# Later loads in the first modulation, its scale and shift on ScalarE, and the spatial weights turned after the feature group

## The chip, the core and the metric

The kernel runs on one core of a Trainium2 chip. The metric is the device time of one execution in microseconds. An execution is one launch of one program, so everything below happens inside one timeline that the hardware profiler can record.

## What is computed

Two blocks run one after the other on a token matrix x of 512 tokens by 2048 features. Only the head of the first block matters here:

```python
cond = jax.nn.silu(c)
mod = cond @ w_ada[l] + b_ada[l]
shift, scale, gate = jnp.split(mod, 3, axis=-1)
h = rms_norm(x, norm_g[l]) * (1.0 + scale[:, None, :]) + shift[:, None, :]
z = h @ w_in[l]
u_a, v_a, g_a, q_b, k_b, v_b, g_b, f_b = jnp.split(z, pts, axis=-1)
y_a = chunked_spatial_gating(gelu(u_a), gelu(v_a), ln_v_g[l], ln_v_b[l], w_s[l], b_s[l]) * silu(g_a)
y_b = forgetting_attention(q_b, k_b, v_b, f_b, b_f[l]) * silu(g_b)
```

`chunked_spatial_gating` multiplies the normalised v_a by the lower triangle of `w_s` (8 heads of 128 by 128). All of this is float32.

## The kernel before

The program is written by hand for each engine. Engines meet at named semaphores, so the order of the code is the order on each engine. SyncE (SP in the profile) issues most loads, in order, into one DMA queue. GpSimd (POOL) issues the weights of the value features v_a. ScalarE (ACT) issues twelve small loads of vectors, the row loads, at the very start.

**Start.** x comes in by tokens. TensorE (PE) turns it by 128 by 128 transposes, ScalarE copies the result into `Y`, squares it, and TensorE sums the squares with a matrix of ones (`norm_squares`). VectorE (DVE) makes the variance from that, ScalarE takes Ln and Exp of it (`norm`), which gives the inverse deviation of every token (semaphore `deviation`).

**Four slabs.** Scale and shift of 2048 features are made in four slabs of 512. For one slab VectorE accumulates 16 blocks of `w_ada` of 512 KB, each times one element of silu(c) (`accumulate`, semaphore `acc_step`). The blocks pass through a ring of six slots in the `arena` (`start_in_0` to `start_in_5`). TensorE sums over the partitions (`reduce_slab`). VectorE turns that into columns (`slab_columns`). Then four tiles of x, already times the inverse deviation (`slab_normed`), get scale and shift (`slab_modulated`, semaphore `modulated`). TensorE multiplies each such tile by the value weights as soon as it is there (`value_product`), 32 float32 products for a slab, while VectorE accumulates the next slab. ScalarE rounds the tiles to `op_hi`, VectorE subtracts to get `op_lo` (`slab_low`): the later products run in three passes over these halves.

**Behind the slabs.** VectorE accumulates one more part of the modulation out of the same ring, 16 steps (`part_tile`), from 8 blocks of 512 KB. ScalarE rounds the first four weight tiles of the group f (a product 112 columns wide that holds the forget logits), and behind that applies Gelu to the value features, which empties the PSUM banks that f writes into. Then TensorE runs the group f, then q (two groups of 512 columns), k, v and the rest.

SyncE's queue around this place holds, in order: the last two `part_tile` blocks, `b_f`, a store of 4096 KB of x (`x_spill`), the bias `b_s`, and the weight blocks of f.

Constants come in one table `const` of 128 by 1408 floats. Its first 256 columns are the identity and the ones; the others, the triangles among them, are used later. `w_s`, its eight transposes and its mask (`tri_le`) stand inside slab 0, and so do the level masks (`masks`).

Of the kernel before, what the change touches and what calls it, by code (L numbers as in the profile page):

```python
# [5 lines left out]
P = 128  # L6
# [179 lines left out]
N_CONST = 7 * P + S  # L186

TMP = 0
AT_X_TOK, AT_START, AT_WS_RAW = 0, 8192, 16384
AT_RSTD_X, AT_PARK = 6144, 6656  # L190
START_RING, SLABS, SLAB = 6, 4, 4
AT_VA, AT_K, AT_V, AT_WST, AT_BS, AT_F, AT_FQ = 2048, 6144, 10240, 14336, 15360, 16384, 16896
# [15 lines left out]
class Build:  # L208
# [56 lines left out]
    def sem(self, name):  # L265
        if name not in self.sems:
            self.sems[name] = self.nc.alloc_semaphore(name)
        return self.sems[name]
# [21 lines left out]
def slab_input(B, slab):  # L290

    return B.at(TMP if slab % 2 else AT_VA, SLAB, S)
# [26 lines left out]
def sync_program(B, sp):  # L319
    A, sem, at = B.A, B.sem, B.at  # L320


    sp.dma_start(B.const[:, :], A["const"]).then_inc(sem("const_in"), 16)


    sp.dma_start(at(AT_X_TOK, NT, D), A["x"][0].rearrange("(n p) d -> p n d", p=P)).then_inc(sem("x_in"), 16)
# [3 lines left out]
    for n in range(SLABS * KT):  # L330
        slab, kt = divmod(n, KT)
        if n >= START_RING:

            sp.wait_ge(sem("acc_step"), n - START_RING + 1)
        sp.dma_start(ring[:, n % START_RING, :, :], w_ada[:, kt, 0:2, slab * GC:(slab + 1) * GC])\
            .then_inc(B.start_in[n % START_RING], 16)
        if n == 3:
            sp.dma_start(at(AT_WS_RAW, HEADS_A, P), A["w_s"][0].rearrange("h t s -> t h s")).then_inc(sem("ws_in"), 16)

            sp.dma_start(B.a_raw[:, :, :, :].rearrange("p a b c -> p (a b c)")[:, 0:len(LEVELS) * P],  # L340
                         A["masks"]).then_inc(sem("masks_in"), 16)
    w_part = A["w_ada"][0].rearrange("(k p) n -> p k n", p=P)
    c = GROUPS[FIRST["f"]]["part"] * GC
    for m in range(KT // 2):
        n = SLABS * KT + m
        if m < START_RING:

            sp.wait_ge(sem("acc_step"), n - START_RING + 1)
        else:

            sp.wait_ge(sem("part_tile"), 2 * (m - START_RING) + 2)
        sp.dma_start(ring[:, n % START_RING, :, :], w_part[:, 2 * m:2 * m + 2, c:c + GC])\
            .then_inc(B.start_in[n % START_RING], 16)
    sp.dma_start(B.bf[96:112, :], A["b_f"].rearrange("o h -> h o")).then_inc(sem("bf_in"), 16)

    sp.wait_ge(sem("x_turned"), KT)
# [240 lines left out]
def pool_program(B, pool):  # L597
    nc, sem, at = B.nc, B.sem, B.at

    pool.wait_ge(sem("acc_step"), 6)  # L600
    for b in range(4 * SLABS):
        g, kt = va_block(b)
        if b >= RAW:

            pool.wait_ge(sem("va_used"), b - RAW + 1)
        pool.dma_start(B.w_raw[:, b % RAW, :, :],
                       B.weight(GROUPS[g])[:, kt:kt + 2, GROUPS[g]["col"]:GROUPS[g]["col"] + GC])\
            .then_inc(B.va_in[b % RAW], 16)

    queries = at(AT_QST, 2, S)  # L610

    pool.wait_ge(sem("mixing"), HEADS_A)
    for h in range(HEADS_B):
        rows, others = (slice(DH_B * (x % 2), DH_B * (x % 2 + 1)) for x in (h, h + 1))
        if h < 2:
            nc.gpsimd.memset(queries[others, h, :], 0.0)
        if h >= 2:

            pool.wait_ge(sem("scores"), 4 * (h - 1) + 1)
        nc.gpsimd.tensor_copy(queries[rows, h % 2, :], B.Y[rows, 8 + h // 2, :])  # L620
        nc.gpsimd.drain().then_inc(sem("queries_in"), 1)

    n = FIRST["wo1"]

    pool.wait_ge(B.bank_free[n % 2], n // 2 + 1)
    nc.gpsimd.memset(at(AT_WGC, 1, 2048)[0:33, 0, :], 0.0)
    nc.gpsimd.drain()
    nc.gpsimd.memset(B.arena[32:33, AT_RC:AT_RC + SC], 1.0)
    nc.gpsimd.drain()
    nc.gpsimd.memset(B.small[0:1, 95:96], 0.0).then_inc(sem("gates_cleared"), 1)  # L630

    pool.wait_ge(sem("states_out"), 1)
    nc.gpsimd.memset(at(AT_WG, 1, 512)[0:33, 0, :], 0.0)
    nc.gpsimd.drain()
    nc.gpsimd.memset(B.arena[32:33, AT_RT:AT_RT + S], 1.0)
    nc.gpsimd.drain()
    nc.gpsimd.memset(B.small[0:1, 95:96], 0.0).then_inc(sem("gates_cleared"), 1)
# [36 lines left out]
def scalar_program(B, act):  # L674
# [273 lines left out]
    for slab in range(SLABS):  # L948
        for t in range(SLAB):
            k = SLAB * slab + t  # L950
            act.wait_ge(sem("modulated"), k + 1)
            Act(B.op_hi[:, k, :], slab_input(B, slab)[:, t, :], ACT.Copy).then_inc(sem("op_high"), 1)
    for c in range(4):
        high_tile(c, GROUPS[FIRST["f"]]["width"])

# [327 lines left out]
def tensor_program(B, pe):  # L1283
# [262 lines left out]
    for t in range(KT):  # L1546
# [2 lines left out]
        for j in range(NT):  # L1549
            last = turn(ps[:, 1 + t % 4, j * P:(j + 1) * P], x_tok[:, j, t * P:(t + 1) * P])  # L1550
        last.then_inc(sem("turned"), 1)
    pe.wait_ge(sem("ws_in"), 16)
    for h in range(HEADS_A):
        last = turn(ps[:, 5 + h // 4, h % 4 * P:(h % 4 + 1) * P], at(AT_WS_RAW, HEADS_A, P)[:, h, :])
    last.then_inc(sem("ws_turned"), 1)
    norm_squares()

    def reduce_slab(slab):
# [15 lines left out]
                  B.w_raw[:, b % RAW, k, :], start=t % SLAB == 0 if own else t == 0,  # L1574
                  stop=t % SLAB == SLAB - 1 if own else t == KT - 1)

    pe.wait_ge(sem("ws_masked"), 1)
    reduce_slab(0)
    for slab in range(SLABS):

# [21 lines left out]

    F = FIRST
    group(F["f"])
    run(F["q"], 1)
    run(F["k"], 1)
    run(F["v"], 1)
    mixer_tensor(B, pe, reduce_parts)
# [237 lines left out]
def vector_program(B, dve):  # L1846
# [401 lines left out]
    def slab_columns(slab):  # L2248


        dve.wait_ge(sem("start_summed"), slab + 1)
        k = SLAB * slab
        bias = B.vec[:, VEC["b_ada"]:VEC["b_ada"] + 32].rearrange("p (v c) -> p v c", v=2)[:, :, k:k + SLAB]
        mod = B.mod[:, 0:32].rearrange("p (v c) -> p v c", v=2)[:, :, k:k + SLAB]
        V.tensor_tensor(mod, ps[:, 7, 0:2 * SLAB].rearrange("p (v c) -> p v c", v=2), bias, ALU.add)
        V.drain()
        V.scalar_tensor_tensor(out=B.mod[:, 16 + k:16 + k + SLAB], in0=B.mod[:, 16 + k:16 + k + SLAB], scalar=1.0,
                               in1=B.vec[:, VEC["norm_g"] + k:VEC["norm_g"] + k + SLAB], op0=ALU.add, op1=ALU.mult)
        V.drain()

    def slab_normed(slab):

# [3 lines left out]
        V.tensor_tensor(slab_input(B, slab), Y[:, SLAB * slab:SLAB * slab + SLAB, :],  # L2266
                        at(AT_RSTD_X, 1, S).to_broadcast([P, SLAB, S]), ALU.mult)
        V.drain()

    def slab_modulated(slab):  # L2270
        x = slab_input(B, slab)
        for t in range(SLAB):
            k = SLAB * slab + t
            V.tensor_scalar(x[:, t, :], x[:, t, :], B.mod[:, 16 + k:17 + k], B.mod[:, k:k + 1],  # L2274
                            ALU.mult, ALU.add).then_inc(sem("modulated"), 1)

    def slab_low(slab, t):
        k = SLAB * slab + t
# [16 lines left out]
    for n in range(SLABS * KT):  # L2295
        slab, kt = divmod(n, KT)
        accumulate(n)
        if slab == 0:
            if kt == 9:
                dve.wait_ge(sem("ws_turned"), 1)  # L2300
                V.tensor_tensor(at(AT_WST, HEADS_A, P), ps[:, 5:7, :].rearrange("p b (h t) -> p (b h) t", t=P),
                                B.tri_le.unsqueeze(1).to_broadcast([P, HEADS_A, P]), ALU.mult).then_inc(sem("ws_masked"), 1)
            if kt == 11:
                dve.wait_ge(sem("masks_in"), 16)
                V.tensor_copy(B.masks[:, :, :].rearrange("p l c -> p (l c)"),
                              B.a_raw[:, :, :, :].rearrange("p a b c -> p (a b c)")[:, 0:len(LEVELS) * P])\
                    .then_inc(sem("masks_made"), 1)
            if kt == 12:
                dve.wait_ge(sem("squares_summed"), 4)
                V.tensor_scalar(at(AT_RSTD_X, S), ps[:, 7, :], 1.0 / D, EPS, ALU.mult, ALU.add)\  # L2310
                    .then_inc(sem("variance"), 1)
            if kt == 14:
                dve.wait_ge(sem("deviation"), 1)
                slab_normed(0)
        else:
            if kt == 1:
                slab_columns(slab - 1)
                slab_modulated(slab - 1)
            if kt in (4, 5, 6, 7):
                slab_low(slab - 1, kt - 4)  # L2320
            if kt == 15:
                park(slab - 1)
                slab_normed(slab)
    slab_columns(SLABS - 1)
    slab_modulated(SLABS - 1)
    for t in range(SLAB):
        slab_low(SLABS - 1, t)

    for t in range(KT):
        part_tile(FIRST["f"], t)  # L2330
    park(SLABS - 1)

    def scaled(m):
# [11 lines left out]
    for n, g in enumerate(GROUPS):  # L2345
# [22 lines left out]
        if name == "f":  # L2368

            for k in range(FIRST["va"], FIRST["va"] + 2):  # L2370
                dve.wait_ge(B.bank_free[k % 2], k // 2 + 1)
            stats = B.small[:, 16:16 + 48].rearrange("p (a s) -> p a s", s=12)
            for b in range(NT):
                for h in range(2):
                    V.bn_stats(stats[:, b, 6 * h:6 * h + 6], va[:, b, h * GC:(h + 1) * GC])
            V.drain()
            for b in range(NT):
                V.bn_aggr(B.small[:, 64 + 2 * b:66 + 2 * b], stats[:, b, :])
            V.drain()
            mv = B.small[:, 64:72].rearrange("p (a b) -> p a b", b=2)  # L2380
            V.tensor_scalar(B.small[:, 0:4], mv[:, :, 1], EPS, None, ALU.add).then_inc(sem("value_variance"), 1)
        if name == "q" and i == 0:
            dve.wait_ge(sem("value_deviation"), 1)
            V.reciprocal(B.small[:, 4:8], B.small[:, 0:4])
# [431 lines left out]
```

## Time and profile before

| | us |
|---|---|
| median of 3 runs | 2897.32 |
| lowest and highest of them | 2896.2, 2901.43 |
| the profiled execution's own time | 2894.05 |
| span of its trace | 2892.3 |
| TensorE busy in the span | 2774.3 |
| VectorE busy | 1791.3 |
| ScalarE busy | 1047.8 |

The span runs from the first to the last instruction of the program in the trace; the time of the execution has a little around it. All later times are microseconds from the start of the span. In a row of the timeline the first number is the start, the second the duration of the row (it can hold several instructions, xN), and the brackets at the end say how long the engine was idle before it and what ended that. A `q` behind an engine's name means its sequencer, that is, the issue of a transfer.

### The profile page before, as it was taken

How to read it: one execution, taken by the hardware profiler on the slowest of the kernel's cores; microseconds unless marked ns; L12 is line 12 of the kernel's file. 1: busy time of each engine (PE TensorE's matmuls, PEld its weight loads, DVE VectorE, ACT ScalarE, POOL GpSimd, SP SyncE). 2: the span in 40 equal slices, each digit the busy share in tenths (PEclk: the TensorE clock that was granted, in tenths of full speed). 3: DMA queues.
4: the chain of work that ended last, by engine and by line, in shares of the span. 5: the costliest groups of instructions: out<-in, count | busy, mean ns of one | idle time of the engine just before them, and what ended most of it. 6: DMA issues, size and time to landing. Idle time of an engine off the chain costs nothing.

```text
span 2892.3 us, 35101 instructions
## 1 busy us (share of the span) xinstructions
PE 2774.3 (96%) x12345; PEld 2198.7 (76%) x12345; DVE 1791.3 (62%) x2747; ACT 1047.8 (36%) x1633; POOL 27.4 (1%) x44
## 2 busy tenths in 40 slices
PE   6999999999999989999999999999999899999996
PEld 3468887777788866788877778787788688888884
DVE  6856675555698757455564738483977776335454
ACT  3032222444332364422243534443422622234224
POOL 0000000000000000000000000000000000000000
PEclk9999999999999999999999999999999999999998
DMA  9966552222466647466522322235566365333341
GB/s 344 356 211 216 190 190 90 79 75 73 145 205 201 221 139 255 142 212 194 193 69 88 95 79 87 73 94 179 192 228 218 108 212 189 95 99 99 124 124 58
DMA packets 240189, 451.25 MB, mean 156 GB/s; under 512 B 23848, under 2 KB 45818, under 8 KB 235436
## 3 DMA queue, kind: packets, MB, share of 16 engines
q1 hardware_dynamic: 237236, 440.80, 46.4%
q0 software_dynamic: 2304, 8.39, 0.8%
q8 instruction: 86, 1.41, 0.2%
q14 instruction: 59, 0.48, 0.1%
q10 hardware_dynamic: 504, 0.17, 0.0%
HBM read 422.01 MB, written 27.30 MB: 155 GB/s over the span
## 4 chain that ended last, share of the span: by engine, by line
PE 74%; issue 13%; DVE 5%; ACT 2%; DVEq 2%; DMA 1%; ACTq 1%; SPq 1%; POOLq 0%; POOL 0%
PE ps L1345 18%; PE ps L1348 18%; PE ps L1351 18%; PE ps L1573 3%; PE ps L1801 2%; PE ps L1358 1%; PE ps L1364 1%; PE ps L1361 1%; PE ps L1718 1%; PE ps L1709 1%; PE ps L1832 1%; PE ps L1835 1%; PE ps L1315 1%; PE ps L1320 1%; PE ps L1317 1%
## 5 line engine op out<-in xcount | busy, mean ns | idle before, releaser
L1345 PE MATMUL ps<-op_hi,w_hi 128*128 128x512 f32 (+2 forms) x2800 | 782.8, 399 | 21.2 <-ACT op_hi L926 8.2
L1858 DVE TENSOR_TENSOR w_lo<-w_raw,w_hi 128x512 fp32r<-128x512 f32 (+2 forms) x672 | 440.6, 661 | 555.0 <-ACT w_hi L688 307.5
L1351 PE MATMUL ps<-op_hi,w_lo 128*128 128x512 f32 (+2 forms) x2800 | 756.3, 390 | 4.4 <-DVE w_lo L1858 4.4
L1348 PE MATMUL ps<-op_lo,w_hi 128*128 128x512 f32 (+2 forms) x2800 | 759.5, 391 | 0.0
L1345 PEld LDWEIGHTS ps<-op_hi,w_hi 128*128 128x128 f32 (+1 forms) x2800 | 519.7, 190 | 138.2 <-issue 23.2
L1351 PEld LDWEIGHTS ps<-op_hi,w_lo 128*128 128x128 f32 (+1 forms) x2800 | 527.8, 189 | 116.2 <-DVE w_lo L1858 5.6
L1348 PEld LDWEIGHTS ps<-op_lo,w_hi 128*128 128x128 f32 (+1 forms) x2800 | 529.8, 189 | 112.7 <-issue 0.3
L688 ACT ACTIVATE w_hi<-w_raw 128x512 fp32r<-128x512 f32 (+2 forms) x416 | 242.8, 592 | 607.2 <-PE ps L1351 446.9
L713 ACT ACTIVATE w_hi<-w_raw 128x512 fp32r<-128x512 f32 x288 | 181.8, 632 | 580.9 <-PE ps L1351 451.4
L1881 DVE SCALAR_TENSOR_TENSOR acc<-a_raw,vec,acc 128x512 f32<-128x512 f32 x525 | 381.5, 745 | 15.3 <-DMA a_raw<-in_w_ada 12.3
L2586 DVE TENSOR_TENSOR w_lo<-w_raw,w_hi 128x512 fp32r<-128x512 f32 x128 | 83.5, 686 | 63.8 <-ACT w_hi L1208 58.4
L1358 PE MATMUL ps<-w_hi,op_hi 128*128 128x512 f32 x384 | 111.6, 399 | 4.2 <-ACT w_hi L688 4.2
L1573 PE MATMUL ps<-w_raw,arena 128*128 128x512 f32 x256 | 112.4, 600 | 1.1 <-DVE arena L2274 1.1
L1364 PE MATMUL ps<-w_lo,op_hi 128*128 128x512 f32 x384 | 109.2, 393 | 2.7 <-DVE w_lo L1858 2.6
L1361 PE MATMUL ps<-w_hi,op_lo 128*128 128x512 f32 x384 | 108.6, 391 | 0.0
L1573 PEld LDWEIGHTS ps<-w_raw,arena 128*128 128x128 f32 x256 | 49.0, 193 | 61.4 <-issue 59.4
L2510 DVE TENSOR_TENSOR w_lo<-w_raw,w_hi 128x512 fp32r<-128x512 f32 x64 | 44.3, 692 | 76.1 <-ACT w_hi L1116 76.1
L1244 ACT ACTIVATE arena<-arena 128x2048 f32<-128x2048 f32 x28 | 53.6, 1915 | 101.5 <-DVE arena L2639 101.5
L1358 PEld LDWEIGHTS ps<-w_hi,op_hi 128*128 128x128 f32 x384 | 71.5, 189 | 23.1 <-ACT w_hi L688 5.5
L1208 ACT ACTIVATE w_hi<-w_raw 128x512 fp32r<-128x512 f32 x128 | 75.3, 621 | 36.1 <-PE ps L1351 36.1
L1364 PEld LDWEIGHTS ps<-w_lo,op_hi 128*128 128x128 f32 x384 | 71.8, 188 | 20.3 <-DVE w_lo L1858 5.4
L1361 PEld LDWEIGHTS ps<-w_hi,op_lo 128*128 128x128 f32 x384 | 72.4, 189 | 15.6
(279 smaller groups left out, 2413.8 us busy)
## 6 DMA issues: line engine op xcount, KB each, us to landing
a_raw<-in_w_ada SPq DMA_DIRECT2D x216, 512.0 KB, 4.0
w_raw<-in_w_in_e SPq DMA_DIRECT2D x160, 512.0 KB, 4.7
w_raw<-in_w_in SPq DMA_DIRECT2D x96, 512.0 KB, 4.8
arena<-in_w_ada SPq DMA_DIRECT2D x72, 512.0 KB, 6.9
w_raw<-in_w_in_o SPq DMA_DIRECT2D x64, 512.0 KB, 4.3
w_raw<-in_w_out SPq DMA_DIRECT2D x32, 512.0 KB, 4.9
w_raw<-in_w_out_e SPq DMA_DIRECT2D x32, 512.0 KB, 5.0
w_raw<-in_w_out_o SPq DMA_DIRECT2D x32, 512.0 KB, 3.8
```

Of the source, the lines that this page charges most:

```text
L688: Act(B.w_hi[:, c % RING, 0:width], B.w_raw[:, raw, c % 2, 0:width], ACT.Copy).then_inc(sem("hi_done"), 1)
L713: Act(B.w_hi[:, t % RING, 0:width], B.w_raw[:, raw, t % 2, 0:width], ACT.Copy).then_inc(sem("hi_done"), 1)
L1345: mm(ps[0:m, bank + j, 0:tok], hi[:, cols], B.op_hi[:, k, 0:tok], start=first, stop=False)
L1348: mm(ps[0:m, bank + j, 0:tok], hi[:, j * P:j * P + m], B.op_lo[:, k, 0:tok], start=False, stop=False)
L1351: last = mm(ps[0:m, bank + j, 0:tok], lo[:, j * P:j * P + m], B.op_hi[:, k, 0:tok], start=False, stop=last_t)
L1358: mm(ps[:, bank + j, :], B.op_hi[:, k, rows], hi, start=first, stop=False)
L1361: mm(ps[:, bank + j, :], B.op_lo[:, k, j * P:j * P + P], hi, start=False, stop=False)
L1364: last = mm(ps[:, bank + j, :], B.op_hi[:, k, j * P:j * P + P], lo, start=False, stop=last_t)
L1573: return mm(ps[:, 4 * g + j, :], slab_input(B, slab)[:, t % SLAB, j * P:(j + 1) * P], B.w_raw[:, b % RAW, k, :], start=t % SLAB == 0 if ow ...
L1858: V.tensor_tensor(B.w_lo[:, c % RING, 0:width], B.w_raw[:, c // 2 % RAW, c % 2, 0:width], B.w_hi[:, c % RING, 0:width].bitcast(f32), ALU.s ...
L1881: last = V.scalar_tensor_tensor(out=sums, in0=x, scalar=col, in1=sums, op0=ALU.mult, op1=ALU.add)
L2586: V.tensor_tensor(B.w_lo[:, c % RING, :], B.w_raw[:, c // 2 % RAW, c % 2, :], B.w_hi[:, c % RING, :].bitcast(mybir.dt.float32), ALU.subtract)\
```

## The change

Four things are changed. (1) Of `const` only the first 256 columns come first; `masks`, the rest of `const` and `w_s` are issued behind the eight `part_tile` blocks, and `w_s` waits on SyncE for the tenth `part_tile`, since it now lies in a slot of the ring. (2) GpSimd issues the third and fourth value weight block of the first slab only after eleven accumulations. (3) Scale and shift of the slab tiles go from VectorE to ScalarE, in the same instruction stream as the rounding. (4) The transposes of `w_s` stand between f and q on TensorE, its mask on VectorE behind the statistics of the value features, and the copy of the level masks behind the `part_tile` steps.

```diff
@@ sync_program
-    sp.dma_start(B.const[:, :], A["const"]).then_inc(sem("const_in"), 16)
+    sp.dma_start(B.const[:, 0:2 * P], A["const"][:, 0:2 * P]).then_inc(sem("const_in"), 16)
...
-        if n == 3:
-            sp.dma_start(at(AT_WS_RAW, HEADS_A, P), A["w_s"][0].rearrange("h t s -> t h s")).then_inc(sem("ws_in"), 16)
-
-            sp.dma_start(B.a_raw[:, :, :, :].rearrange("p a b c -> p (a b c)")[:, 0:len(LEVELS) * P],
-                         A["masks"]).then_inc(sem("masks_in"), 16)
...
+    sp.dma_start(B.a_raw[:, :, :, :].rearrange("p a b c -> p (a b c)")[:, 0:len(LEVELS) * P],
+                 A["masks"]).then_inc(sem("masks_in"), 16)
+    sp.dma_start(B.const[:, 2 * P:], A["const"][:, 2 * P:]).then_inc(sem("const_rest_in"), 16)
+
+    sp.wait_ge(sem("part_tile"), 10)
+    sp.dma_start(at(AT_WS_RAW, HEADS_A, P), A["w_s"][0].rearrange("h t s -> t h s")).then_inc(sem("ws_in"), 16)
     sp.dma_start(B.bf[96:112, :], A["b_f"].rearrange("o h -> h o")).then_inc(sem("bf_in"), 16)
@@ pool_program
+        if b == 2:
+            pool.wait_ge(sem("acc_step"), 11)
@@ scalar_program
             k = SLAB * slab + t
-            act.wait_ge(sem("modulated"), k + 1)
-            Act(B.op_hi[:, k, :], slab_input(B, slab)[:, t, :], ACT.Copy).then_inc(sem("op_high"), 1)
+            x = slab_input(B, slab)[:, t, :]
+            if t == 0:
+                act.wait_ge(sem("slab_ready"), slab + 1)
+            Act(x, x, ACT.Identity, scale=B.mod[:, 16 + k:17 + k], bias=B.mod[:, k:k + 1]).then_inc(sem("modulated"), 1)
+            nc.scalar.drain()
+            Act(B.op_hi[:, k, :], x, ACT.Copy).then_inc(sem("op_high"), 1)
@@ tensor_program
-    pe.wait_ge(sem("ws_in"), 16)
-    for h in range(HEADS_A):
-        last = turn(ps[:, 5 + h // 4, h % 4 * P:(h % 4 + 1) * P], at(AT_WS_RAW, HEADS_A, P)[:, h, :])
-    last.then_inc(sem("ws_turned"), 1)
...
-    run(F["q"], 1)
+
+    pe.wait_ge(sem("const_rest_in"), 16)
+    pe.wait_ge(sem("ws_in"), 16)
+    for h in range(HEADS_A):
+        last = turn(ps[:, 1 + h // 4, h % 4 * P:(h % 4 + 1) * P], at(AT_WS_RAW, HEADS_A, P)[:, h, :])
+    last.then_inc(sem("ws_turned"), 1)
+    group(F["q"])
+    pe.wait_ge(sem("ws_masked"), 1)
+    group(F["q"] + 1)
@@ vector_program
-            if kt == 9:
-                dve.wait_ge(sem("ws_turned"), 1)
-                V.tensor_tensor(at(AT_WST, HEADS_A, P), ps[:, 5:7, :].rearrange("p b (h t) -> p (b h) t", t=P),
-                                B.tri_le.unsqueeze(1).to_broadcast([P, HEADS_A, P]), ALU.mult).then_inc(sem("ws_masked"), 1)
...
             if kt == 1:
                 slab_columns(slab - 1)
-                slab_modulated(slab - 1)
...
+            dve.wait_ge(sem("const_rest_in"), 16)
+            dve.wait_ge(sem("ws_turned"), 1)
+            V.tensor_tensor(at(AT_WST, HEADS_A, P), ps[:, 1:3, :].rearrange("p b (h t) -> p (b h) t", t=P),
+                            B.tri_le.unsqueeze(1).to_broadcast([P, HEADS_A, P]), ALU.mult).then_inc(sem("ws_masked"), 1)
```

On SyncE, this is what is issued from the `part_tile` blocks of the ring on, before the change; the brackets hold the semaphores that an issue waits for.

```order
L352 DMA arena<-in_w_ada 128x2x512 [waits part_tile] x2
L354 DMA bf<-in_b_f 16x1
L357 DMA x_spill<-Y 128x8192 [waits x_turned]
L534 DMA arena<-in_b_s 128x1024 [waits acc_step]
L377 DMA w_raw<-in_w_in 128x2x112 [waits va_used] x4
```

And this is the same place after the change.

```order
L347 DMA arena<-in_w_ada 128x2x512 [waits part_tile] x2
L349 DMA a_raw<-in_masks 128x896
L351 DMA const<-in_const 128x1152
L354 DMA arena<-in_w_s 128x8x128 [waits part_tile]
L355 DMA bf<-in_b_f 16x1
L358 DMA x_spill<-Y 128x8192 [waits x_turned]
L535 DMA arena<-in_b_s 128x1024 [waits acc_step]
L378 DMA w_raw<-in_w_in 128x2x112 [waits va_used] x4
```

Three loads have moved in ahead of the store `x_spill` and of the weights of f, and one of the three holds a wait of its own, behind which all the others stand.

On ScalarE, this is the handling of a slab's tiles and what follows the last one, before the change.

```order
L952 ACTIVATE op_hi<-arena 128x512 [waits modulated] x16
L688 ACTIVATE w_hi<-w_raw 128x112 [waits weights_in_0]
...
L688 ACTIVATE w_hi<-w_raw 128x112 [waits weights_in_1]
...
L972 ACT_TABLE_LOAD
L972 ACTIVATE arena<-ps 128x4x512 [waits va_used]
```

After the change one slab reads like this on ScalarE (three more slabs follow, then the same rows for w_hi and the Gelu).

```order
L957 ACTIVATE arena<-arena,mod 128x512 [waits slab_ready]
L959 ACTIVATE op_hi<-arena 128x512
L957 ACTIVATE arena<-arena,mod 128x512
L959 ACTIVATE op_hi<-arena 128x512
L957 ACTIVATE arena<-arena,mod 128x512
L959 ACTIVATE op_hi<-arena 128x512
L957 ACTIVATE arena<-arena,mod 128x512
L959 ACTIVATE op_hi<-arena 128x512
```

Sixteen instructions have come over to ScalarE, each followed by a drain and the rounding of the same tile; the Gelu still stands behind the first weight tiles of f.

## Rows read from the trace of the kernel before

**Rows 1.** The page: busy time of each engine and its share.

```profile
PE 2774.3 (96%) x12345; PEld 2198.7 (76%) x12345; DVE 1791.3 (62%) x2747; ACT 1047.8 (36%) x1633; POOL 27.4 (1%) x44
```

**Rows 2.** The timeline from the start to the first value product.

```profile
6.54 5.28 SPq L338 DMA_DIRECT2D arena<-in_w_s  x1
...
16.18 0.81 PE L1289 MATMUL ps<-const,Y 128*128 128x128 f32 x3 [16.18 <-DMA Y<-in_pool_scale]
...
16.79 10.19 PE L1289 MATMUL ps<-const,arena 128*128 128x128 f32 x72
...
29.12 14.00 PE L1440 MATMUL ps<-arena,const 128*128 128x512 f32 x32 [2.14 <-ACT arena L809]
...
33.67 1.22 DVE L2301 TENSOR_TENSOR arena<-ps,const 128x1024 f32<-128x1024 f32 x1
...
43.16 0.69 DVE L2310 TENSOR_SCALAR arena<-ps 128x512 f32<-128x512 f32 x1
...
44.59 2.67 DVE L2245 SCALAR_TENSOR_TENSOR acc<-arena,vec,acc 128x1024 f32<-128x1024 f32 x2 [0.73 <-DMA arena<-in_w_ada]
45.86 0.63 ACT L816 ACTIVATE arena<-arena 128x512 f32<-128x512 f32 x1
47.18 2.28 DVE L2266 TENSOR_TENSOR arena<-Y,arena 128x2048 f32<-128x2048 f32 x1
...
50.99 3.54 PE L1302 MATMUL ps<-const,acc 128*128 128x1 f32 x16 [7.87 <-DVE acc L2245]
...
55.66 4.80 PE L1573 MATMUL ps<-w_raw,arena 128*128 128x512 f32 x7 [1.13 <-DVE arena L2274]
```

**Rows 3.** Busy time by stretch: engines, granted clock, DMA share, GB/s.

```profile
20.00:40.00 20.00, 17.86 (x84) 11.64 (x84) 14.52 (x12) 15.71 (x20) 3.01 (x4) 1.00 1.06 379
...
55.66:82.19 26.53, 26.52 (x59) 11.78 (x60) 23.52 (x23) 2.18 (x4) 2.17 (x3) 0.94 0.89 315
```

**Rows 4.** The second slab in the timeline; the groups of 0 to 250 us.

```profile
83.89 27.71 PE L1573 MATMUL ps<-w_raw,arena 128*128 128x512 f32 x64
...
L2274 DVE TENSOR_SCALAR arena<-arena,mod 128x512 f32<-128x512 f32 x16 | 7.7, 542 | 0.3
```

**Rows 5.** The timeline of ScalarE and TensorE at a later modulation.

```profile
2272.76 0.81 ACT L924 ACTIVATE arena<-Y,mod 128x512 f32<-128x512 f32 x1 [2.38 <-DVEq L2136]
...
2274.27 0.81 ACT L924 ACTIVATE arena<-Y,mod 128x512 f32<-128x512 f32 x1
...
2274.42 2.04 PE L1345 MATMUL ps<-op_hi,w_hi 128*128 128x512 f32 x4 [8.19 <-ACT op_hi L926]
2276.26 1.63 PE L1348 MATMUL ps<-op_lo,w_hi 128*128 128x512 f32 x4
```

**Rows 6.** The timeline from the last slab to group f, one DMA issue among it.

```profile
144.89 2.49 DVE L1995 TENSOR_TENSOR op_lo<-arena,op_hi 128x512 fp32r<-128x512 f32 x4
...
147.90 12.72 DVE L1881 SCALAR_TENSOR_TENSOR acc<-arena,vec,acc 128x512 f32<-128x512 f32 x15
...
151.31 0.42 SPq L357 DMA_DIRECT2D x_spill<-Y  x1
...
w_raw<-in_w_in SPq DMA_DIRECT2D x1, 112.0 KB, 15.7
...
167.92 0.85 ACT L688 ACTIVATE w_hi<-w_raw 128x112 fp32r<-128x112 f32 x4 [22.09 <-DMA w_raw<-in_w_in]
...
170.09 1.88 ACT L972 ACTIVATE arena<-ps 128x2048 f32<-128x2048 f32 x1
...
172.12 0.79 PE L1345 MATMUL ps<-op_hi,w_hi 128*112 128x512 f32 x1
```

**Rows 7.** The timeline of TensorE and VectorE in the first group of q.

```profile
185.32 1.15 PE L1345 MATMUL ps<-op_hi,w_hi 128*128 128x512 f32 x4 [1.63 <-issue]
...
196.95 0.69 DVE L1858 TENSOR_TENSOR w_lo<-w_raw,w_hi 128x512 fp32r<-128x512 f32 x1
...
198.10 1.07 PE L1351 MATMUL ps<-op_hi,w_lo 128*128 128x512 f32 x4
```

More of the change, by code:

```diff
@@ L188 @@
 TMP = 0
-AT_X_TOK, AT_START, AT_WS_RAW = 0, 8192, 16384
+AT_X_TOK, AT_START, AT_WS_RAW = 0, 8192, 10240
 AT_RSTD_X, AT_PARK = 6144, 6656
@@ L1575, in value_product @@
                   stop=t % SLAB == SLAB - 1 if own else t == KT - 1)
-    pe.wait_ge(sem("ws_masked"), 1)
     reduce_slab(0)
@@ L2258, in slab_columns @@
                                in1=B.vec[:, VEC["norm_g"] + k:VEC["norm_g"] + k + SLAB], op0=ALU.add, op1=ALU.mult)
-        V.drain()
+        V.drain().then_inc(sem("slab_ready"), 1)
     def slab_normed(slab):
@@ L2268, in slab_normed @@
         V.drain()
[L2270 to L2275, printed above, removed]
     def slab_low(slab, t):
@@ L2298, in vector_program @@
         if slab == 0:
-            if kt == 9:
-                dve.wait_ge(sem("ws_turned"), 1)
-                V.tensor_tensor(at(AT_WST, HEADS_A, P), ps[:, 5:7, :].rearrange("p b (h t) -> p (b h) t", t=P),
-                                B.tri_le.unsqueeze(1).to_broadcast([P, HEADS_A, P]), ALU.mult).then_inc(sem("ws_masked"), 1)
[L2303 to L2307, printed above, removed]
             if kt == 12:
@@ L2324, in vector_program @@
     slab_columns(SLABS - 1)
-    slab_modulated(SLABS - 1)
     for t in range(SLAB):
@@ L2330, in vector_program @@
         part_tile(FIRST["f"], t)
+    dve.wait_ge(sem("masks_in"), 16)
+    V.tensor_copy(B.masks[:, :, :].rearrange("p l c -> p (l c)"),
+                  B.a_raw[:, :, :, :].rearrange("p a b c -> p (a b c)")[:, 0:len(LEVELS) * P])\
+        .then_inc(sem("masks_made"), 1)
     park(SLABS - 1)
```

## The prediction, made before the changed kernel was run

> **What bounds the kernel now.** I read the page first, to see whose time counts. TensorE is busy for 96% of the span [rows 1], so a change at the head can only move the end if it moves TensorE's work or opens a gap in it. The timeline of the head then shows where TensorE waits. It waits for the row loads until 16.18. It transposes x with no idle time ahead, so x had landed. From 29.12 it sums the squares for 14.00 us, and from 43.12 it idles 7.87 us until the last accumulation of slab 0 is done [rows 2]. Its first value product starts at 55.66 [rows 2]. From there on it does not stop: a slab takes 27.71 us of products with nothing between [rows 4], until the group f at 172.12 [rows 6].
>
> Two places therefore decide: the start of the products (55.66), and the start of f, which needs two things at once, the end of the products and the Gelu (170.09 plus 1.88 is 171.97). The Gelu stands on ScalarE behind four weight tiles of f, and ScalarE waited 22.09 us for those weights [rows 6]. Both conditions are met in the same microsecond before the change. So f has no slack on either side: products that end sooner bring nothing unless the weights of f come sooner, and later weights cost in full.
>
> **The start of the products.** `const` shrinks from 1408 to 256 columns of floats: 128 x 1152 x 4 bytes, 0.59 MB, no longer travel ahead of x. At 379 GB/s [rows 3] that is 1.5 us. The rest that leaves the head (`masks`, `w_s`) was queued behind x and the first four blocks and does not touch x.
>
> The chain from x to the variance is serial: transposes, copies, squares, sums (14.00), variance at 43.16, and Exp until 46.49 (45.86 plus 0.63). All of it shifts by 1.5, so Exp would end at 44.99. VectorE's own side: from the variance (43.16) to `slab_normed` (47.18) it spent 4.02 us, of which 0.73 waited for a block [rows 2]. With blocks that land sooner this is 3.3, so from 41.66 it is ready at about 45.0. Both give 45.1 in place of 47.18, a gain of 2.1. The mask of `w_s` (1.22 us at 33.67 [rows 2]) and the copy of the masks leave VectorE in a stretch where it would wait for the sums of squares anyway. They gain nothing, and the same holds for the eight transposes of `w_s`: the squares on ScalarE end after them. Were the sums of squares not in the way, the accumulations alone could be done some 10 us sooner; they are in the way.
>
> GpSimd's new wait holds two blocks of value weights back until the eleventh accumulation. The eleventh is due near 34 us (from about 18, at 2.67/2 each [rows 2], with a little for the first two blocks of weights beside them), and the two are needed 14 us (half of 27.71) into the first slab, near 68. I cost it at nothing; the 34 us between are the cover.
>
> A point of doubt is whether the row loads move too, since TensorE waited for them, not for x. They are twelve small loads, and they were still under way while 4 MB of x passed. I take it that they are slow because they share the engines with x, so that they end sooner when x does. If they stay at 16.18, nothing ahead of Exp moves, and the gain is only VectorE's wait: 47.18 less 46.49, 0.7. The Trainium skill, DMA: Bandwidth & Descriptors, section "Issuing engines are not separate DMA queues", says that loads from all issuing engines run on the same 16 DMA engines and interleave. By that rule the row loads move with x, and the sum stays as I have it.
>
> **Scale and shift on ScalarE.** VectorE took 542 ns for a tile [rows 4]. The same form on ScalarE, Identity with a scale and a bias from the modulation table, takes 0.81 us, and with the drain and the rounding a tile comes every 1.51 us (2272.76 to 2274.27) [rows 5]. TensorE waits for the first tile of slab 0, so this costs 0.27 there: the first product starts at 55.66 - 2.1 + 0.27 = 53.8. In the later slabs TensorE still has three products of the old slab (six records of 27.71/64 = 0.43, 2.6 us) while the columns are made, so 0.27 is mostly hidden; I take 0.1 for each of three. A tile every 1.51 us is enough, since TensorE works 3.5 us on one (8 records). So the products end 1.5 us sooner than before (2.1 - 0.27 - 0.3). The Trainium skill, ScalarE: Activation LUTs, section "Rules for kernel authors", says that add and mul belong on VectorE and not on ScalarE. By that rule the move costs and brings nothing; the rows make it 0.27 at the start and the next item behind the last slab.
>
> VectorE is freed of 4 x 0.54 us a slab, but it is not the bound in the slabs: TensorE is. After the last slab it is worse off. `slab_low` ended at 147.38 (144.89 plus 2.49) [rows 6]. Now its fourth tile waits for ScalarE. The columns are ready at about 143.0, since the old modulated tiles began there (144.89 less 3 x 0.54, rounded down for the overlap). The fourth rounding ends 3 x 1.51 + 0.81 + 0.07 + 0.63 = 6.0 us later, at 149.1, and 0.7 of subtraction follows: 149.8. So `part_tile` starts 2.4 us later relative to the products.
>
> **The queue ahead of f.** This is the large term. Before, SyncE issued `x_spill` at 151.31, and the weights of f came 16.6 us later, at 167.92, behind 4 MB of `x_spill` and 0.5 MB of `b_s` in the same queue [rows 6]. Now SyncE waits for ten `part_tile` steps first. The fifteen steps after the first took 12.72 us from 147.90, 0.85 each, so the tenth ended at 147.90 + 9 x 0.85 = 155.5; with the 2.4 us it is 157.9. Then `w_s`, `b_f` and `x_spill` are issued, each at about 0.45: `x_spill` at 158.8, which is 7.5 us later. `masks` and the rest of `const` (1.05 MB, 2.8 us at 379 GB/s) go into the queue near 153 and are through by then. What stands ahead of f's weights is then one block of 0.5 MB (`w_s` in place of the last block of `w_ada`), `x_spill` and `b_s`, the same bytes as before. So f's weights come 16.6 us after `x_spill` again: 7.5 us later relative to the products. The lower end is 5, if the store runs faster with the queue to itself. The upper end comes from `w_s`: its issue took 5.28 us at the head [rows 2], where the queue was full; if that were the issue's own cost, 7.5 would be 12.
>
> Rounding, table load and Gelu follow unchanged, so f starts at 172.12 + 7.5 - 1.5 = 178.1. TensorE has meanwhile idled some 7 to 8 us. After a gap of 8.19 us at 2274.42 the first four products took 2.04 us and the next four 1.63 [rows 5], against 1.07 in the steady run [rows 7]: 1.5 us lost to the lower clock. In slab 0 the granted clock was 0.94 over 26.53 us [rows 3], 12% of it at half speed, 1.6 lost. I add 1.5, with 0 to 1.6 as ends for its size.
>
> **Between f and q.** TensorE idled 1.63 us before q at 185.32 [rows 7], waiting for weights that are issued at f's pace, so this gap moves along. Eight transposes (10.19/72 = 0.14 each, 1.1 us [rows 2]) fit into it; `w_s` landed long before. Without that cover they would cost 1.1. The mask, 1.22 us, now precedes the low tile that VectorE starts at 196.95 and ends at 197.64. TensorE needs it at 198.10 [rows 7]: slack 0.46, so 0.76 is lost. The copy of the masks lies in a stretch in which VectorE has nothing to do.
>
> **The sum**, against the profiled execution's 2894.05: -1.5 (products sooner) + 7.5 (f's weights) + 1.5 (clock) + 0.8 (mask) = +8.3, which gives 2902.4. The median of the runs is 2897.32, 3.3 above the profiled one, so I predict 2905.6.
>
> **Rivals.**
> (a) The store absorbs most of it. If the 4 MB drain sooner and the clock stays up, the terms are -2 + 5 + 0 + 0.5 = +3.5: 2901. For it: the queue is emptier when the store is issued. Against: the same bytes took 16.6 us.
> (b) The weights of f do not gate, and only the head counts: -1.5 + 0.8 = -0.7, 2896.6. Against it stands ScalarE's wait of 22.09 us that ended on just these weights.
> (c) Faster. The sums of squares do not hold the first slab, and the accumulations set the start, 10 us sooner, and VectorE's lead pulls `part_tile` along: -10 - 1.5 + 7.5 - 2 = -6, 2891. It decides when the variance is ready before 35 us; 14.00 us of products after 27 speak against it.
> (d) The issue of `w_s` costs 5 us by itself: +13, 2910.
> (e) The row loads stay at 16.18: the gain at the start shrinks by 1.4 and the sum becomes +9.7, 2907.
>
> **Chances.** The forecast 0.47, (e) 0.13, (d) 0.09, (a) 0.18, (b) 0.09, (c) 0.04. A measurement tells 0.2%, 5.8 us, from no change. Slower by more than that: the forecast, (d) and (e), less a little for the forecast's lower edge: 0.66. Within: (a), (b) and that edge, 0.29. Faster: 0.05. The range from 2898 to 2912 leaves out (b) and (c) and the far end of (d).
>
> **What the profile would show.** First value product near 53.8, with its modulated tile from ScalarE at 0.81 us each. No new wait in slabs 1 to 3. `x_spill` issued near 157.3 (158.8 less 1.5). A gap on TensorE of 7 to 8 us before f, ended by the Gelu, with the clock at its lower level behind it. A short wait of TensorE for a low tile in the first q group. I am wrong if f starts before 174, or if f's weights come clearly less than 16.6 us after `x_spill` is issued.

## The result and the profile after

The changed kernel took 2908.68 us (median of 6 runs, 2905.67 to 2909.66), the kernel before 2898.16 (6 runs, 2896.04 to 2903.93): a ratio of 1.0027, 95% interval 1.0017 to 1.0037. It is slower by 7.8 us by the ratio (0.0027 x 2898) and by 10.5 by the medians; forecast were 2905.6 and 8.3. The profiled execution after took 2905.67 at a span of 2903.9, against 2894.05 at 2892.3.

The first two groups are the page after, busy time of each engine, and the timeline of TensorE and ScalarE from the start to the first value product.

```profile
PE 2781.0 (96%) x12345; PEld 2199.8 (76%) x12345; DVE 1784.4 (61%) x2731; ACT 1060.9 (37%) x1649; POOL 27.4 (1%) x44
```

```profile
15.29 0.81 PE L1296 MATMUL ps<-const,Y 128*128 128x128 f32 x3 [15.29 <-DMA Y<-in_pool_scale]
...
27.84 14.00 PE L1447 MATMUL ps<-arena,const 128*128 128x512 f32 x32 [3.09 <-ACT arena L812]
...
49.01 3.58 PE L1309 MATMUL ps<-const,acc 128*128 128x1 f32 x16 [7.17 <-DVE acc L2255]
53.10 0.81 ACT L957 ACTIVATE arena<-arena,mod 128x512 f32<-128x512 f32 x1 [7.89 <-DVEq L2269]
53.97 28.22 PE L1576 MATMUL ps<-w_raw,arena 128*128 128x512 f32 x58 [1.38 <-ACT arena L957]
```

The row loads ended 0.89 sooner than in [rows 2], the sums of squares began 1.28 sooner, and the first value product stands at 53.97 in place of 55.66: the head gave 1.7. It was soon lost. Busy time by stretch, after (in a row: the stretch and its length; busy us and instructions of PE, PEld, DVE, ACT and POOL; granted clock; DMA share; GB/s):

```profile
46.00:60.00 14.00, 9.61 (x23) 6.01 (x24) 11.65 (x13) 5.45 (x8) 0.00 (x0) 0.52 0.78 251
53.97:82.03 28.06, 28.06 (x59) 12.25 (x60) 21.56 (x20) 4.64 (x7) 2.17 (x3) 0.89 0.94 325
```

The same stretch before:

```profile
46.00:60.00 14.00, 7.88 (x23) 5.51 (x24) 11.75 (x14) 2.69 (x5) 0.00 (x0) 0.63 0.82 287
```

The clock has two levels, full and half, so a granted clock of 0.52 over 14 us is 13.4 us at the lower one (2 x 0.48 x 14), and 0.63 is 10.4. The products start sooner and run slower, so the first slab, 26.53 us in [rows 3], takes 28.06, and the lead is down to 0.15. Nothing stalls in slabs 1 to 3; the last column sums begin at 140.55 (140.69 before).

This belongs to the one execution and not to the change. Four kernels below have the same code up to this place. All four read 0.63 in this stretch, as before; in three the last column sums begin at 138.66, 138.93 and 139.57, and only the fourth lost its lead too (140.83), in its sums of squares, which took 15.70 us in place of 14.00.

Now the part that decides. The timeline after, from the last slab to q, of TensorE, ScalarE, VectorE and the issues on SyncE:

```profile
140.55 1.84 PE L1309 MATMUL ps<-const,acc 128*128 128x1 f32 x16
142.91 0.81 ACT L957 ACTIVATE arena<-arena,mod 128x512 f32<-128x512 f32 x1 [22.45 <-DVEq L2269]
148.05 0.63 ACT L959 ACTIVATE op_hi<-arena 128x512 fp32r<-128x512 f32 x1
148.71 0.69 DVE L2005 TENSOR_TENSOR op_lo<-arena,op_hi 128x512 fp32r<-128x512 f32 x1 [0.72 <-ACT op_hi L959]
149.90 12.72 DVE L1891 SCALAR_TENSOR_TENSOR acc<-arena,vec,acc 128x512 f32<-128x512 f32 x15
152.81 0.46 SPq L349 DMA_DIRECT2D a_raw<-in_masks  x1
153.32 0.43 SPq L351 DMA_DIRECT2D const<-in_const  x1
157.52 0.38 SPq L354 DMA_DIRECT2D arena<-in_w_s  x1
158.69 0.42 SPq L358 DMA_DIRECT2D x_spill<-Y  x1
159.65 25.49 SPq L378 DMA_DIRECT2D w_raw<-in_w_in  x8
175.30 0.85 ACT L691 ACTIVATE w_hi<-w_raw 128x112 fp32r<-128x112 f32 x4 [26.63 <-DMA w_raw<-in_w_in]
177.47 1.88 ACT L979 ACTIVATE arena<-ps 128x2048 f32<-128x2048 f32 x1
179.40 0.77 PE L1352 MATMUL ps<-op_hi,w_hi 128*112 128x512 f32 x1 [6.86 <-ACT arena L979]
192.33 1.03 PE L1296 MATMUL ps<-const,arena 128*128 128x128 f32 x8
193.64 1.16 PE L1352 MATMUL ps<-op_hi,w_hi 128*128 128x512 f32 x4 [0.28 <-issue]
```

ScalarE's last rounding ends at 148.68 and `part_tile` starts at 149.90, 2.0 later than in [rows 6]. SyncE stands from 153.75 (the issue of `const`) to 157.52 for the tenth `part_tile`. `x_spill` goes out at 158.69 and f's weights reach ScalarE at 175.30, 16.6 us later, as before (151.31 to 167.92). TensorE idles 6.86 ahead of f, and q starts 8.32 later than in [rows 7]. The issues of the stretch 150 to 161, with the time from issue to landing:

```profile
x_spill<-Y SPq DMA_DIRECT2D x1, 4096.0 KB, 14.6
arena<-in_w_ada SPq DMA_DIRECT2D x2, 512.0 KB, 5.4
const<-in_const SPq DMA_DIRECT2D x1, 576.0 KB, 8.6
arena<-in_w_s SPq DMA_DIRECT2D x1, 512.0 KB, 6.0
...
a_raw<-in_masks SPq DMA_DIRECT2D x1, 448.0 KB, 7.7
w_raw<-in_w_in SPq DMA_DIRECT2D x1, 112.0 KB, 15.6
```

`masks` landed at 160.5 and the rest of `const` at 161.9, not ahead of the store but about 2 and 3 us behind its issue. Behind q the difference between the two traces wanders between 8.3 and 14.7 us, in both directions, at steps where the granted clock changes in the one and not in the other, and ends at 11.6.

In the tables below, "to f" and "to q" are the times from the start of the last column sums to the first product of f and of q; this takes the head, and what its clock did, out of the comparison. "Gap" is TensorE's idle time ahead of f. Each ratio is against the kernel before, measured beside the kernel in question. Before: 31.43 to f (172.12 - 140.69), 44.63 to q. After: 38.85 and 53.09, gap 6.86.

### The profile page after: what moved, and what is told of

Its sections match the earlier page's. It is cut to its first block, busy times and chain, and to the rows that moved or that the text cites. A ratio compares the mean times of both kernels' runs of the same rounds, so it can differ in the third digit from the quotient of the medians.

```text
span 2903.9 us, 35121 instructions
## 1 busy us (share of the span) xinstructions
PE 2781.0 (96%) x12345; PEld 2199.8 (76%) x12345; DVE 1784.4 (61%) x2731; ACT 1060.9 (37%) x1649; POOL 27.4 (1%) x44
## 4 chain that ended last, share of the span: by engine, by line
PE 85%; DVE 5%; ACT 3%; issue 2%; DMA 2%; ACTq 2%; DVEq 2%; SPq 0%
PE ps L1352 21%; PE ps L1355 20%; PE ps L1358 20%; PE ps L1576 3%; PE ps L1365 2%; PE ps L1371 2%; PE ps L1368 2%; PE ps L1811 2%; PE ps L1845 1%; PE ps L1842 1%; PE ps L1322 1%; PE ps L1327 1%; PE ps L1324 1%; PE ps L1728 1%; PE ps L1719 1%
## 5 line engine op out<-in xcount | busy, mean ns | idle before, releaser
L1891 DVE SCALAR_TENSOR_TENSOR acc<-a_raw,vec,acc 128x512 f32<-128x512 f32 x525 | 381.3, 745 | 17.9 <-DMA a_raw<-in_w_ada 15.3
```

The lines of the kernel that those rows point to most:

```text
L1891: last = V.scalar_tensor_tensor(out=sums, in0=x, scalar=col, in1=sums, op0=ALU.mult, op1=ALU.add)
```

## The experiments

Two causes could make f's weights late, and the expectations weigh them. One is the wait, the step of the prediction: SyncE stands for the tenth `part_tile` and all behind it stands too. The other is the bytes: `masks`, the rest of `const` and `w_s`, 1.5 MB, now travel between the last blocks and f's weights, and a store issued sooner would end no sooner. A third part is ScalarE's tiles, which start `part_tile` later.

**The wait behind the store** (changed kernel; `w_s` and its wait go behind `x_spill` and `b_s`).

```diff
-    sp.wait_ge(sem("part_tile"), 10)
-    sp.dma_start(at(AT_WS_RAW, HEADS_A, P), A["w_s"]...)
     ...  # b_f, x_spill, b_s
+    sp.wait_ge(sem("part_tile"), 10)
+    sp.dma_start(at(AT_WS_RAW, HEADS_A, P), A["w_s"]...)
```

> The changed kernel with w_s and its wait for the tenth part_tile moved behind x_spill and b_s in SyncE's order. Theory A (the wait on SyncE holds the store back, and f's weights with it): x_spill is issued right after the rest of const, near 154.7 instead of 158.7; masks, the rest of const and w_s (1.5 MB) are still ahead of f's weights, so these land near 173 instead of 175.3, f starts near 177, and the time falls by 1.5 to 3 us from 2908.7. Theory B (the bytes of the three loads in the queue are the whole cost, the wait is harmless): f's weights land at 175 as before and the time does not move.

Ratio 1.0029 (1.0019 to 1.0038): nothing gained. The issues of its stretch 145 to 165:

```profile
x_spill<-Y SPq DMA_DIRECT2D x1, 4096.0 KB, 17.8
...
w_raw<-in_w_in SPq DMA_DIRECT2D x1, 112.0 KB, 17.9
```

The store was issued at 154.54, 4.15 sooner, and took 17.8 us in place of 14.6, so it landed only 0.9 sooner (172.3 and 173.3). `w_s`, issued at 157.80 and now behind it, landed 17.9 us later, at 175.7, and f's weights right behind at 176.1. It was 39.42 to f. Without the wait the bytes hold f, and the wait as the one cause has fallen.

**The store early** (changed kernel; `x_spill` is issued ahead of the last two `part_tile` blocks, where SyncE would next wait for a slot of the ring).

```diff
+        if m == START_RING:
+            sp.wait_ge(sem("x_turned"), KT)
+            sp.dma_start(B.x_sp, B.Y[:, :, :]).then_inc(sem("spilled"), 16)
...
-    sp.wait_ge(sem("x_turned"), KT)
-    sp.dma_start(B.x_sp, B.Y[:, :, :]).then_inc(sem("spilled"), 16)
```

> The changed kernel with the 4 MB store x_spill issued before the seventh part_tile block, near 136, in place of behind w_s. Theory A (f's weights behind the store are the whole loss of about 8 us): f's weights land before 166, the idle time of TensorE before f goes to about 0, the clock stays at its full level there, and the time is 2898 to 2900, about that of the kernel before. Rival C (ScalarE's modulated tiles and the later mask cost several us by themselves): f starts on time but the time stays above 2903. Rival D (the store takes the DMA engines from the value weights of the last slab): a wait of TensorE for w_raw inside slab 3 of several us.

Ratio 1.0002 (0.9991 to 1.0013). Its timeline at the end of SyncE's program for the slabs:

```profile
150.92 0.47 SPq L352 DMA_DIRECT2D a_raw<-in_masks  x1
...
155.64 0.38 SPq L357 DMA_DIRECT2D arena<-in_w_s  x1
...
157.36 18.03 SPq L379 DMA_DIRECT2D w_raw<-in_w_in  x8
```

The wait and the 1.5 MB are still there, but 4 MB no longer stand behind them. f's first weights were issued at 157.36 and reached ScalarE at 162.69, well ahead of need. f started with no gap ahead of it, 32.37 to f: 6.5 of the 7.4 us are back, and the ratio is clear of that of the changed kernel. So nearly all the loss lies in when the store's bytes leave.

Of the 0.94 that is left, 0.70 is a new wait inside the last slab, the expectation's rival D in small. TensorE waited for a block of value weights, which GpSimd had issued at 134.95, 0.6 behind the store (134.34), and which took 15.7 us to land:

```profile
150.76 20.84 PE L1577 MATMUL ps<-w_raw,arena 128*128 128x512 f32 x48 [0.70 <-DMA w_raw<-in_w_in]
...
167.00 0.48 ACT L692 ACTIVATE w_hi<-w_raw 128x112 fp32r<-128x112 f32 x2 [3.82 <-DMA w_raw<-in_w_in]
```

The second row shows a condition of f that the prediction does not have: ScalarE needs four weight tiles of f ahead of the Gelu, and the third and fourth came only at 167.00. The next experiment shows why.

**The same on the kernel before**, a control: does an early store help by itself?

> The kernel before with the same early store and nothing else. By theory A f had no slack before but was not late either, so the time is that of before within 1 us (2897 to 2899): the products still end at 172. If it is several us faster, the store gated something in the kernel before as well; if slower, the store costs where it now stands, and e2 has to be read with that.

Ratio 1.0002 (0.9994 to 1.0011), 31.42 to f. It does not. The first two tiles came early, at 162.84, and the other two as before: 27.33 us behind the column sums (169.31 - 141.98), against 27.23 in the kernel before, where all four were taken at 167.92.

```profile
169.31 0.48 ACT L689 ACTIVATE w_hi<-w_raw 128x112 fp32r<-128x112 f32 x2 [5.99 <-DMA w_raw<-in_w_in]
```

Their load goes into a slot that the value products free. What SyncE waits for between 120 and 200 us says so, here in the kernel before:

```profile
SPq L377 <- PE ps L1573: 18.2, 2, 12.2
```

So with the store out of the way the products set f twice over: directly, and by this slot. The early store repairs what the change broke, and nothing else.

**Scale and shift back on VectorE** (changed kernel; `slab_modulated` returns to VectorE, which is not shown in the cut).

```diff
-            if t == 0:
-                act.wait_ge(sem("slab_ready"), slab + 1)
-            Act(x, x, ACT.Identity, scale=B.mod[:, 16 + k:17 + k], bias=B.mod[:, k:k + 1])...
-            nc.scalar.drain()
-            Act(B.op_hi[:, k, :], x, ACT.Copy).then_inc(sem("op_high"), 1)
+            act.wait_ge(sem("modulated"), k + 1)
+            Act(B.op_hi[:, k, :], slab_input(B, slab)[:, t, :], ACT.Copy).then_inc(sem("op_high"), 1)
```

> The changed kernel with scale and shift of the slab tiles back on VectorE. Theory A: the first product starts 0.2 us sooner, part_tile starts 1.9 us sooner behind the last slab, so x_spill and f's weights come 1.9 us sooner, and the time falls by about 2 us, to 2906 to 2907. Rival: if VectorE's relief in the slabs mattered, a wait of TensorE appears in slabs 1 to 3 and the time rises.

Ratio 1.0021 (1.0011 to 1.0031). 36.10 to f, 2.75 less than after. The store went out at 155.26, measured from the column sums 2.2 sooner than after (15.94 against 18.14). The tiles on ScalarE thus cost 2.75 of the 7.4 us, 2.2 of it in the place that the prediction named. This rests on the traces: the intervals of the two ratios (1.0021 and 1.0027) overlap. No new wait appeared in slabs 1 to 3, so VectorE's relief was worth nothing there.

**The loads ahead** (changed kernel; `masks` and the rest of `const` ahead of the last two blocks, the wait stays), and **both** (with the edit of the first experiment too).

```diff
+        if m == START_RING:
+            sp.dma_start(B.a_raw...[:, 0:len(LEVELS) * P], A["masks"]).then_inc(sem("masks_in"), 16)
+            sp.dma_start(B.const[:, 2 * P:], A["const"][:, 2 * P:]).then_inc(sem("const_rest_in"), 16)
...
-    sp.dma_start(B.a_raw...[:, 0:len(LEVELS) * P], A["masks"]).then_inc(sem("masks_in"), 16)
-    sp.dma_start(B.const[:, 2 * P:], A["const"][:, 2 * P:]).then_inc(sem("const_rest_in"), 16)
```

> The changed kernel with masks and the rest of const issued ahead of the seventh part_tile block, where the DMA engines were idle (145 to 150 us); w_s, its wait and x_spill stay. Measured from the last column sum (L1309, slab 3) to f's first product, which takes out what the clock did earlier: 31.4 us in the kernel before, 38.9 in the changed one. Theory B (the 1.5 MB more in the queue are the whole delay): 1.05 MB less at some 300 GB/s, f 3.5 us sooner, 35.4. Theory AB (the bytes and SyncE's wait each bind by themselves, so that removing one shows the other): x_spill is still issued near 158.7 and f's weights come 15 to 16.6 us later, 37.5 to 38.9.

> e5 and e1 together: masks and the rest of const ahead, the wait and w_s behind x_spill and b_s. Both theories leave only w_s (0.5 MB) and ScalarE's late tiles (part_tile 1.9 us later): f's weights 3.7 us sooner than in the changed kernel, 35.1 us from the last column sum to f, and a gap of TensorE of 3 to 4 us. If it stays near 38 to 39, neither the bytes nor the wait are the cause.

The loads ahead alone: 1.0024 (1.0015 to 1.0033), 37.18 to f. Both: 1.0011 (1.0002 to 1.0021), 35.59. In the first the store was issued at 156.95 behind the wait, 18.0 us behind the column sums as after (18.14), and took 13.3. So the wait removed alone gives nothing, the loads removed alone 1.7, both 3.3. Of these 3.3 us the bytes by themselves hold all, the wait by itself half: the expectation that each binds alone (37.5 to 38.9 to f) was nearly met.

**All three** (both, and scale and shift on VectorE).

> The changed kernel with the three repairs that leave the store where it is: masks and the rest of const ahead of the last blocks, w_s and its wait behind the store, scale and shift on VectorE. From the start of the last column sums to the first product of f it took 31.43 us before the change, 38.85 after it, 35.59 with the first two repairs, 36.10 with the third alone. If ScalarE's later tiles and the queue add up (they held up the store one behind the other), this is 35.6 less 2.75, near 32.8, where the 1.4 left is w_s ahead of f's weights, and the ratio is near 0.9995. If ScalarE's part was only the wait for the tenth step, which is gone from this place already, it stays near 35.6 and the ratio near 1.001.

Ratio 0.9999 (0.9990 to 1.0008), 33.43 to f: 5.4 of the 7.4 us are back, where 3.3 and 2.75 make 6.0, so the parts nearly add. The store now left when it did before, 10.63 us behind the column sums against 10.62, and took 14.7 us. Most of the 2.0 left is `w_s`, which now stands between `b_s` and f's weights: `b_s` landed at 166.0 (149.94 + 16.1) and `w_s` at 167.8 (153.67 + 14.1), 1.7 us apart.

**VectorE for the tiles, and the store early.**

> The changed kernel with the early store of e2 and scale and shift back on VectorE. f's weights are early in both, so ScalarE's later tiles cost only 0.24 us at the first product and nothing behind the last slab: 31.4 to 32.4 us from the last column sum to f as in e2, and the time of e2 within 1 us (2898). If it is 2 us or more faster than e2, the move to ScalarE costs in a place not seen.

> The fastest kernel again, on one chip with the one beside it: scale and shift on VectorE and the store ahead of the last blocks. If its first result was its time and not chance, ratio 0.9987 with 0.001 to either side, and 31.4 us from the last column sums to f.

2896.3 (2892.19 to 2899.03) against 2899.78, ratio 0.9987 (0.9978 to 0.9996), the fastest of all. The repeat gave 2895.88 and 0.9991 (0.9981 to 1.0001). It was 31.43 and 31.42 to f. This version keeps the head's gain and pays nothing for it; that it beats the kernel before by about 0.1% is likely, though the repeat's interval just reaches 1. Its expectation took 2 us or more over the early store alone as a sign that the tiles on ScalarE cost in a place not seen. The medians are 2.2 apart (2898.5 and 2896.3), but of different sets, and the intervals overlap, so the times do not decide it. The traces show 0.94 to f: TensorE's wait of 0.70 in the last slab is gone. The likely reason is the order of two issues: with the store early alone the store went out 0.6 us ahead of that block of value weights, which took 15.7 us; here it went out 1.1 and 1.7 us behind it (136.64 behind 135.53, and 137.10 behind 135.35), and the block took 8.4 and 7.6. The first products, in the repeat's timeline:

```profile
49.10 3.58 PE L1306 MATMUL ps<-const,acc 128*128 128x1 f32 x16 [7.18 <-DVE acc L2252]
53.80 2.93 PE L1573 MATMUL ps<-w_raw,arena 128*128 128x512 f32 x3 [1.13 <-DVE arena L2281]
```

**The same with seven more products behind the sums of squares**, to keep TensorE busy in its idle stretch; their result isn't used.

```diff
     norm_squares()
+    for _ in range(7):
+        mm(ps[:, 0, :], B.ones, at(AT_SQ, S), start=True, stop=True)
```

> e7 with seven more 128x512 products of the ones on TensorE behind the sums of squares (their result is overwritten): they fill 6 of the 7.2 idle us before the first column sum. If the lower clock there is what cost 3 to 5 us (column sum 3.57 for 1.84, slab 0 at 0.94 or less), the clock stays at its full level, the column sum takes 1.8 us, and slab 0 ends 3 to 4 us sooner: about 2895. If the clock is lowered all the same, no change against e7.

Ratio 0.9993 (0.9984 to 1.0002), the same as without them, so neither branch of the expectation came: the lower clock did not go away, and it was not unchanged. Its stretch was shorter:

```profile
49.00:57.00 8.00, 6.84 (x21) 4.52 (x22) 6.71 (x11) 2.19 (x4) 0.00 (x0) 0.57 0.64 215
```

2 x 0.43 x 8 is 6.9 us at the lower level, against 10.4 before and 13.4 after, and the last column sums came 0.9 sooner than in the kernel that it extends (138.31, 139.24). The times cannot tell 0.9 us from nothing.

| kernel | to f | to q | gap | ratio |
|---|---|---|---|---|
| before | 31.43 | 44.63 | - | 1 |
| after | 38.85 | 53.09 | 6.86 | 1.0027 |
| wait behind the store | 39.42 | 54.17 | 7.43 | 1.0029 |
| loads ahead | 37.18 | 51.48 | 5.18 | 1.0024 |
| scale on VectorE | 36.10 | 51.09 | 4.11 | 1.0021 |
| loads ahead, wait behind | 35.59 | 50.71 | 3.60 | 1.0011 |
| all three | 33.43 | 46.05 | 1.44 | 0.9999 |
| store early | 32.37 | 45.25 | - | 1.0002 |
| before, with the store early | 31.42 | 44.55 | - | 1.0002 |
| scale on VectorE, store early | 31.43 | 44.34 | - | 0.9987 |
| the same again | 31.42 | 44.53 | - | 0.9991 |
| the same, seven more products | 31.43 | 44.44 | - | 0.9993 |

## Why the prediction came out right, and where it was right by luck

**The start of the products: right at 53.97 for 53.8; its worth was given back in this execution.** The row loads ended 0.89 sooner and the sums of squares began 1.28 sooner, so rival (e) did not come true. This agrees in part with the Trainium skill, DMA: Bandwidth & Descriptors, section "Issuing engines are not separate DMA queues", by which loads from all issuing engines share 16 DMA engines: 0.89 of the 1.5 us showed at the row loads. The step that failed in this trace is "So the products end 1.5 us sooner than before". It took the clock's stretch in slab 0 as unchanged; it stayed at the lower level for 13.4 us and not 10.4, and of 1.7 us, 0.15 were left at the last column sums. Of the nine traces with the changed head and no added products, the other eight tell more: in seven (four of them with scale and shift on VectorE) the last column sums begin between 138.66 and 139.57, that is 1.1 to 2.0 us sooner than before, and in one (the wait behind the store) 0.14 later. The second trace of the old head, the kernel before with the store early, has 141.98, 1.3 later than the first. So the term was of the right size, and in some executions the clock takes about as much as it is worth.

**Scale and shift on ScalarE: right.** The pair comes every 1.42 us (1.51 forecast), `part_tile` starts 2.0 later, and relative to the column sums 2.1 (2.4 forecast). That the add and multiply cost when put on ScalarE is shown by moving them back: 2.75 us less to f. The Trainium skill, ScalarE: Activation LUTs, section "Rules for kernel authors", which keeps add and mul on VectorE, agrees with these runs.

**The queue ahead of f: the number right, the mechanism half right.** The forecast had the store's issue and f's weights 7.5 us later relative to the products. Against the column sums the store was issued 7.5 later (18.14 and 10.62), and f came 7.4 later (38.85 - 31.43). The step that failed is "`masks` and the rest of `const` ... are through by then" and the "same bytes as before" that follows from it. They landed at 160.5 and 161.9, behind the store's issue. In the stretch 155 to 160 the queue moved 304 GB/s and not the 379 taken, and the last two blocks of the ring had taken 5.4 us each when the two loads joined them. Beside ScalarE's tiles, the wait was costed as the single cause. It agreed with the measurement because the bytes, which it left out, run side by side with it: without the wait 39.42, without the two loads 37.18, without both 35.59. The forecast also took the store alone to decide when f's weights come; the slot that the value products free stands behind it as a second bound, which does not show in the changed kernel and sets f once the store is early. A sum that takes the later of two causes may well be right and still name a cause whose removal brings nothing. A repair designed from the prediction's text alone, the first experiment, gained nothing.

The busy time by stretch after, for the reading of 304:

```profile
150.00:155.00 5.00, 5.00 (x13) 2.28 (x12) 4.41 (x6) 0.00 (x0) 0.00 (x0) 1.00 0.49 139
155.00:160.00 5.00, 5.00 (x13) 2.16 (x12) 4.45 (x6) 0.00 (x0) 0.00 (x0) 1.00 0.86 304
160.00:165.00 5.00, 5.00 (x13) 2.21 (x12) 2.85 (x5) 0.00 (x0) 0.00 (x0) 1.00 1.14 456
```

**The issue of `w_s`, rival (d): out.** It took 0.38 us, not 5.28. The issue of `masks`, right behind it at the head of the kernel before, took 5.40, and 0.46 in its new place. So the place makes the price and not the load; that a full queue was the reason there is likely and not shown.

```profile
11.86 5.40 SPq L340 DMA_DIRECT2D a_raw<-in_masks  x1
```

**The clock at f: 1.0 to 1.6 us for 1.5.** From f to q it took 14.24 after and 13.20 before; the eight transposes in it (1.3 with their gap, 192.33 to 193.64) replace an idle time of 1.63 in [rows 7], as forecast. With all three repairs, where f ran at the full clock throughout, it took 12.62.

**The mask: costed at 0.8, cost nothing in this trace.** It starts at 201.66 and takes 1.22, and the low tile behind it ends at 206.12, before TensorE wants it at 206.42. In five of the nine other traces of the same order a stall of 0.2 to 0.8 us stood there, as with the wait moved behind the store:

```profile
208.76 1.19 PE L1358 MATMUL ps<-op_hi,w_lo 128*128 128x512 f32 x4 [0.80 <-DVE w_lo L1868]
```

**The sum.** At q the change had cost 8.32 where the working gave 7.5 (-1.5 + 7.5 + 1.5), and with the mask, 0 in place of 0.8, both stand at 8.3. The lead came out 1.35 worse than forecast, f's weights and the clock together 0.5 better (8.5 in place of 9.0), the mask 0.8 better: the errors cancelled, and that was luck.

## What to carry to other kernels

When a store or a load is pushed back behind a wait, look at what else goes into the same queue before it: count bytes from the last landing, not from the last issue, and ask for each cause alone what would remain without it. Put a large store that nothing reads soon ahead of a wait of its issuer for a slot, and look at what it then travels beside; here that undid 6.5 of the 7.4 us to f, and in one trace held a block of weights for 0.7. Before moving a store for the sake of a load, see whether that load waits for a slot as well. A gain at the head of an engine that runs slowly there can be given back by its clock: read what still stands behind its stretch of lower clock, and in more than one execution.

## What the runs showed of the hardware

In these runs a short gap ahead of f did not bring the clock down, and longer ones did. With 1.44 us of idle time ahead of f the granted clock stayed at 1.00 (2.4 GHz); with 3.60 it fell to 0.50 (1.2 GHz) while f ran, as it did with each longer one. The kernel with a gap of 1.44, and then the one with 3.60:

```profile
170.00:175.00 5.00, 3.56 (x14) 2.12 (x14) 0.46 (x2) 4.74 (x7) 0.00 (x0) 1.00 0.32 69
175.00:180.00 5.00, 5.00 (x24) 3.80 (x23) 2.15 (x8) 2.08 (x8) 0.00 (x0) 1.00 0.71 188
```

```profile
170.00:175.00 5.00, 1.57 (x4) 0.38 (x2) 0.87 (x4) 3.94 (x6) 0.00 (x0) 0.89 0.37 84
175.00:180.00 5.00, 4.83 (x12) 3.48 (x13) 0.78 (x3) 2.77 (x6) 0.00 (x0) 0.50 0.04 4
```

A shorter gap did not save its whole length: from f to q it took 15.12 us behind the gap of 3.60 and 14.24 behind 6.86, since more of the lower clock lay over the products and less over the idle time. Of 3.26 us saved ahead of f, 2.38 were left at q. And the moment of an issue mattered less than the bytes ahead of it: the store issued 4.15 us sooner took 3.2 us longer (17.8 and 14.6), behind the same `masks` and `const`.
